# A hybrid decoder block on one core: the first phase of the input projection in five k ranges instead of four

## The reference

```
c_act = silu(c)
mod = c_act @ ada_w[l] + ada_b[l]                  # 2048 x 12288
sh1, sc1, g1, sh2, sc2, g2 = split(mod, 6)
u = rms_norm(x, mix_norm_pre[l]) * (1.0 + sc1) + sh1
proj = u @ w_in                                     # 2048 x 16384
rq, rk, rv, rg, mq, mk, mv, ga, gb = split(proj)
```

## Time and profile before

| | us |
|---|---|
| median of 3 runs | 1830.6 |
| lowest and highest | 1830.5, 5219.44 |
| the profiled execution | 1830.5 |
| its span | 1828.5 |
| its mean granted TensorE clock | 0.996 of full speed |

### The profile page before, as it was taken

One profiled execution on the slowest core, in us unless ns is written; L12 is line 12 of the kernel. 1 busy time (PEld: TensorE's weight loads), 2 busy tenths in 40 slices (PEclk: granted clock), 3 DMA queues, 4 the chain that ended last, 5 costly groups with the idle time before them and its releaser, 6 DMA issues.

```text
span 1828.5 us, 26196 instructions
## 1 busy us (share of the span) xinstructions
PE 1803.9 (99%) x8980; PEld 1530.1 (84%) x8980; DVE 1377.5 (75%) x1973; ACT 857.2 (47%) x991; POOL 189.6 (10%) x269
## 2 busy tenths in 40 slices
PE   8999999999999999999999999999999999999998
PEld 6777888888888888888888878888888888888886
DVE  6998788978888788888997576777777776744555
ACT  4444544444454545463445455444444444444444
POOL 0000022222222222222210000000000000000000
PEclk8999999999999999999999999999999999999999
DMA  9999688978888887879886636555555555555552
GB/s 353 387 387 349 186 272 271 289 236 273 271 259 273 257 288 243 288 234 305 276 272 216 209 119 203 185 184 189 193 191 184 184 191 193 188 187 202 185 196 103
DMA packets 304595, 432.96 MB, mean 237 GB/s; under 512 B 50724, under 2 KB 174292, under 8 KB 303888
## 3 DMA queue, kind: packets, MB, share of 16 engines
q1 hardware_dynamic: 244304, 360.77, 59.7%
q0 software_dynamic: 20736, 67.34, 10.5%
q10 hardware_dynamic: 39488, 3.96, 1.7%
HBM read 429.79 MB, written 2.23 MB: 236 GB/s over the span
## 4 chain that ended last, share of the span: by engine, by line
PE 91%; DVE 5%; DMA 1%; issue 1%; ACT 1%; SPq 0%; DVEq 0%; ACTq 0%
PE ps L929 18%; PE ps L559 12%; PE ps L561 12%; PE ps L560 12%; PE ps L590 10%; PE ps L937 9%; PE ps L995 4%; PE ps L997 4%; PE ps L996 4%; DVE ada_acc L1539 2%; DVE w_low L1440 1%; PE ps L598 1%; DVE ada_acc L1521 1%; DMA stage<-in_w_in 1%; DMA ada_first<-in_ada_w 1%
## 5 line engine op out<-in xcount | busy, mean ns | idle before, releaser
L1440 DVE TENSOR_TENSOR w_low<-stage,w_high 128x1024 fp32r<-128x1024 f32 x608 | 743.0, 1223 | 378.2 <-ACT w_high L1041 363.9
L1041 ACT ACTIVATE w_high<-stage 128x1024 fp32r<-128x1024 f32 x552 | 583.7, 1060 | 724.0 <-PE ps L561 273.8
L559 PE MATMUL ps<-w_high,lhs 128*128 128x512 f32 x992 | 389.6, 393 | 0.0
L561 PE MATMUL ps<-w_high,lhs 128*128 128x512 f32 x992 | 386.3, 389 | 0.0
L560 PE MATMUL ps<-w_low,lhs 128*128 128x512 f32 x992 | 386.1, 389 | 0.0
L929 PE MATMUL ps<-lhs,w_high 128*128 128x512 f32 x1408 | 336.7, 391 | 0.5 <-DVE lhs L1488 0.5
L929 PEld LDWEIGHTS ps<-lhs,w_high 128*128 128x128 f32 x1408 | 258.6, 188 | 50.7 <-DVE lhs L1488 0.8
L543 POOL DMA_DIRECT2D ada_ring<-in_ada_w x256 | 185.1, 723 | 755.6 <-DVE ada_acc L1464 538.3
L1464 DVE SCALAR_TENSOR_TENSOR ada_acc<-ada_ring,c_act,ada_acc 128x256 f32<-128x256 f32 x480 | 230.4, 480 | 18.8 <-DMA ada_ring<-in_ada_w 8.7
L561 PEld LDWEIGHTS ps<-w_high,lhs 128*128 128x128 f32 x992 | 186.2, 188 | 39.1
L560 PEld LDWEIGHTS ps<-w_low,lhs 128*128 128x128 f32 x992 | 186.3, 188 | 38.1
(11 more groups left out here) (211 smaller groups left out, 1485.8 us busy)
## 6 DMA issues: line engine op xcount, KB each, us to landing
stage<-in_w_in SPq DMA_DIRECT2D x100, 1024.0 KB, 7.0
stage<-in_ffn_w_up SPq DMA_DIRECT2D x176, 512.0 KB, 4.3
ada_ring<-in_ada_w POOLq DMA_DIRECT2D x256, 256.0 KB, 5.6
stage<-in_ffn_w_down SPq DMA_DIRECT2D x44, 1024.0 KB, 5.0
ada_first<-in_ada_w SPq DMA_DIRECT2D x64, 512.0 KB, 11.3
stage<-in_w_in SPq DMA_DIRECT2D x56, 512.0 KB, 11.4
stage<-in_ret_w_o SPq DMA_DIRECT2D x16, 1024.0 KB, 6.8
stage<-in_moba_w_o SPq DMA_DIRECT2D x16, 1024.0 KB, 6.9
```

The lines of the kernel that those rows point to most:

```text
L559: pe.matmul(acc, hi, w_high[:, slot, k, :], start=kt == 0, stop=False)
L561: last = pe.matmul(acc, lo, w_high[:, slot, k, :], start=False, stop=kt == KT - 1)
L1041: act.activation(w_high[:, h % 4, :, :], stage[:, slot, 2 * (h % 2):2 * (h % 2) + 2, :], ACT.Copy).then_inc(high_ready, 1)
L1440: dve.tensor_tensor(w_low[:, h % 4, :, :], stage[:, slot, 2 * (h % 2):2 * (h % 2) + 2, :], w_high[:, h % 4, :, :].bitcast(F32), ALU.subtra ...
```

## The change

`FIRST_PAIRS` becomes five ranges of 1, 1, 2, 2 and 2 pairs. The units of work are now (group, range), written out for each stage, so that a streamed group may be visited for a range that was ready earlier, or for two ranges in a row without leaving its bank. `VISITS` lists the thirteen stays of a streamed group in banks 6 and 7 (sixteen before): four first ones, copied by ACT, and nine that DVE adds, in two additions each. The next range's summation stands behind RK0, the last unit of a stage, and the first unit behind it is of an older range. The shift and scale are made one load earlier (3 behind the unit instead of 4). For a range of one pair a step is 512 columns wide with shift and scale together, and a slot holds four row blocks. In the opening the steps are 256 wide and alternate between the shift half and the scale half, except in the last slot, where the shift half comes first; each waits for the last step of its own half. The warm-up products are 4, 1 and 12 instead of 33, 1 and 10.

```diff
-FIRST_PAIRS = ((0, 1), (2, 3), (4, 5), (6, 7))
+FIRST_PAIRS = ((0,), (1,), (2, 3), (4, 5), (6, 7))
 STAGES = len(FIRST_PAIRS)
-FIRST_ORDER = ((0, 1, 2, 3, RV0, RQ0, RK0),) * (STAGES - 1) + ((RV0, 0, 1, RQ0, 2, 3, RK0),)
-SUM_BEHIND = (RQ0,) * (STAGES - 1) + (None,)
+FIRST_ORDER = (((0, 0), (1, 0), (RV0, 0), (2, 0), (RQ0, 0), (RK0, 0)),
+               ((3, 0), (3, 1), (RV0, 1), (0, 1), (RQ0, 1), (RK0, 1)),
+               ((1, 1), (1, 2), (RV0, 2), (2, 1), (2, 2), (RQ0, 2), (RK0, 2)),
+               ((3, 2), (3, 3), (RV0, 3), (0, 2), (0, 3), (RQ0, 3), (RK0, 3)),
+               ((1, 3), (1, 4), (RV0, 4), (0, 4), (RQ0, 4), (3, 4), (2, 3), (2, 4), (RK0, 4)))
+SUM_BEHIND = tuple((RK0, st) for st in range(STAGES - 1)) + (None,)
...
+VISITS = []
+for _i, (_g, _r) in enumerate(FIRST_UNITS):
+    if _g < 4 and (_i + 1 == len(FIRST_UNITS) or FIRST_UNITS[_i + 1][0] != _g):
+        VISITS.append((_g, _r, _i, all(_v[0] != _g for _v in VISITS)))
...
             for slot in range(ada_slots(0)):
-                for part in ((0, 1), (1, 2)) if slot > 4 else ((0, 2),):
-                    for k in range(ada_rows(0)):
-                        yield slot, k, part
+                pieces = [(k, part) for k in range(ada_rows(0)) for part in range(2)]
+                if slot == ada_slots(0) - 1:
+                    pieces.sort(key=lambda piece: piece[1])
+                for k, part in pieces:
+                    yield slot, k, part
...
-                if n == FIRST_END[st, SUM_BEHIND[st]] + 4:
+                if n == FIRST_END[SUM_BEHIND[st]] + 3:
                     return st + 1
...
                 if st and 0 in which:
-                    n_out(4 * st - 1, 0)
+                    done = FIRST_UNITS.index(SUM_BEHIND[st - 1])
+                    n_out(sum(i <= done for _, _, i, _ in VISITS) - 1, 0)
...
-            def first_streamed(n, st, j, summed):
+            def first_streamed(n, i, j, r, summed):
+                begins, ends = FIRST_UNITS[i - 1][0] != j, FIRST_UNITS[i + 1][0] != j
...
-            keep_warm(33)
+            keep_warm(4)
             sum_first(0, (0,))
             keep_warm(1)
             sum_first(0, (1,))
-            keep_warm(10)
+            keep_warm(12)
...
-                    if i == 0:
+                    if row == 0:
                         op = dve.tensor_scalar(acc, block_, c_act[:, 0:1], None, ALU.mult)
                     else:
-                        dve.wait_ge(ada1_step, i)
+                        dve.wait_ge(ada1_step, last[part] + 1)
```

More of the change, by code:

```diff
@@ L413, in prepares_before, with kept_before @@
             for st in range(STAGES - 1):
-                if n == FIRST_END[st, SUM_BEHIND[st]] + 4:
+                if n == FIRST_END[SUM_BEHIND[st]] + 3:
                     return st + 1
             return None
[L418 to L424, removed]
+        def kept_before(n, first):
+            for v, (j, r, _, is_first) in enumerate(VISITS):
+                if is_first == first:
+                    end = FIRST_END[j, r]
+                    if n == end + (3 if len(FIRST_PAIRS[r]) == 2 else 4):
+                        yield v, j, r, 0
                     if n == end + 4:
-                        yield st, j, 1
+                        yield v, j, r, 1
         def scaled_by(pair, t):
@@ L452, in first_ada, with first_load @@
                                      "(k p) n -> p k n", p=P)).then_inc((ada1_in, ada1_scale_in)[which][q % 4], 16)
[L454 removed]
+            def first_load(n, pair, g):
                 wait(sp, split_ready, n - 7)
@@ L468, in _ @@
             for st in range(STAGES):
-                for g in FIRST_ORDER[st]:
-                    for pair in FIRST_PAIRS[st]:
-                        first_load(n, st, pair, g)
+                for g, r in FIRST_ORDER[st]:
+                    for pair in FIRST_PAIRS[r]:
+                        first_load(n, pair, g)
                         st_, ops = ada_ops_behind(n)
@@ L612, in _, with n_out @@
             pe.wait_ge(warm_set, 2)
[L614 to L619, removed]
+            def n_out(v, t):
+                if v >= 0:
+                    is_first = VISITS[v][3]
+                    before = sum(visit[3] == is_first for visit in VISITS[:v])
+                    pe.wait_ge(n_kept if is_first else n_added, 2 * before + t + 1)
             def sum_first(st, which=(0, 1)):
@@ L691, in first_streamed @@
                             last.then_inc(used, 1)
-                    if t == 0:
+                    if t == 0 and ends:
                         last.then_inc(n_first, 1)
@@ L708, in _ @@
             sum_first(0, (1,))
[L709 removed]
+            keep_warm(12)
             n = 0
[L711 to L723 removed]
+            for i, (g, r) in enumerate(FIRST_UNITS):
+                summed = 1 + sum(unit in SUM_BEHIND for unit in FIRST_UNITS[:i])
+                if i == 0:
+                    first_opening()
+                elif g < 4:
+                    first_streamed(n, i, g, r, summed)
+                else:
+                    first_resident(n, r, g)
+                n += len(FIRST_PAIRS[r])
+                if (g, r) in SUM_BEHIND:
+                    sum_first(summed)
             def ret_side(G):
@@ L1523, in opening_ada @@
                     op.then_inc(ada1_step, 1)
+                    last[part] = i
             def first_ada(st, i):
@@ L1555, in add_streamed @@
             def add_streamed(n):
-                for st, j, t in kept_before(n, range(1, STAGES)):
+                for v, j, r, t in kept_before(n, False):
                     if t == 0:
-                        dve.wait_ge(n_first, 4 * st + j + 1)
+                        dve.wait_ge(n_first, v + 1)
                     else:
-                        dve.wait_ge(used, FIRST_END[st, j] + 1)
+                        dve.wait_ge(used, FIRST_END[j, r] + 1)
                     b = gate_b[:, t, j * NC:(j + 1) * NC]
```

66 lines of the change are left out of this document (27 added, 39 removed).

## The result

The changed kernel takes 1833.85 us (median of 20 runs; without one disturbed run they lie between 1832.7 and 1836.0), the kernel before 1830.6 (within 0.6 of each other, one disturbed run aside). The ratio is 1.0019, 95% interval 1.0013 to 1.0025. The predicted time, 1830.2, was 3.65 us off. The difference is small, 0.19%, but its interval excludes no change, so the forecast of no change (0.4 us to the fast side) did not hold. The profiled execution of the changed kernel took 1835.3 us with a span of 1833.3, 4.8 more than the span before.

The account below looks back on a forecast made before the run. DVE's pace bounds the first phase: its work eats the 11.6 us head start, and the phase ends at 211.7 to 212.3 against 212.0. So -0.3 to +0.3 on 1830.5, said as 1830.2 us; 8 in 10 between 1825 and 1835.

Parts of the forecast that it names:

- ledger of DVE: First phase, range by range: DVE's work summed in one line, PE's time beside it; phase ends at 211.7 against 212.0.
- rival (b): Opening and range 1: alternate halves don't hide the dependence, narrow steps cost more; loss 3.5 to 6.4 us, chance 0.15.
- PE's waits on additions: First phase: PE's 3.9 us of waits on L1563 go, and waits on the last accumulation step take their place.
- head start: Opening: first useful product at 32.5 instead of 44.16, 11.6 us earlier, of which nothing is left at the phase's end.
- The matmuls behind it start half as fast, which DVE's own pace hides.: Behind range 2's summation: clock falls after PE's 6.8 us idle; only the slower summation costs, 1.1 us of DVE waiting.
- Both arrive together: Range 4, ahead of the last summation: DVE's last step ends at 160.3, PE is done at 159.9.
- the 0.7 for a late split: Range 4, PE's pairs ahead of the last summation: 0.7 us added for a late split, and 0.7 once more behind it.
- this cover: Behind each summation: RK0 of the same range, 5.4 us, stood there before; now the summation is behind RK0, a new wait.
- the forecast's own range: Whole kernel: 1828.3 us (the clock holds, 1.1 less, gaps smaller) to 1832; forecast's chance 0.55.
- Rival (c): Transfers: 1 KB rows run a fifth lower, 310 GB/s, 5.4 us more, 4 of it covered; 1831.7 us, chance 0.1.
- a last shift row after 165: End of first phase: last shift expected near 162; before 158 or after 165 would show the forecast wrong.
- Rival (a): First phase: the head start stays, 1818.9 us, or some 4 us of it, 1826.5; chance together 0.2.

Follow-up runs that it names:

- c1: Changed kernel with all but the first accumulation step of each range after the opening covering only 128 columns (work left out): 1828.02 us.
- c3: c1 with the scale half of ada_w also neither loaded nor waited for in ranges 2 to 4: 1817.63 us.
- e5: e1 and e3 together on the changed kernel, with 8 zero-matrix filler products ahead of range 1's summation as well: 1831.64 us.
- r1: Changed kernel run again without an edit, for a second profile: 1834.21 us, profiled run 1834.07.
- e1: Changed kernel plus zero-matrix filler products on PE ahead of the summations of range 2 (28) and range 3 (6): 1831.25 us, ratio to before 1.0004.
- e6: Four ranges of two pairs as before, with the new visits, alternating opening and RK0 behind the summation: 1829.58 us, ratio to before 0.9996.
- e3: Changed kernel with partial sums of one-pair visits taken out one load earlier (3 behind instead of 4): 1833.90 us.
- e4: e3 plus the summation moved back behind RQ0, RK0 running behind it, shift and scale again four loads behind: 1833.84 us.
- e7: e6 with DVE's shift and scale made one split earlier (3 behind instead of 4): 1829.42 us, ratio to before 0.9995.

## Why the prediction was wrong

**The opening and the ledger of DVE held.** Forecast against rows: opening's end 27.6, measured 26.87; shift 28.4, 27.57; range 1's shift 52.6, 53.36; range 2's wait of PE 6.8, measured 6.54; its shift 82.2, 83.53; range 3's 121.2, 122.81. The first useful product came at 31.47 for 32.5. The alternating halves hide the dependence, so rival (b) is excluded. PE's waits on additions became the single one ahead of the third summation, as said. One part of the ledger was short: from shift 0 to shift 1 it had 24.2 us and 25.8 passed, 1.2 of the difference being DVE's waits of 0.78 and 0.39 us for ACT's conversions at 40.9 and 46.7. With the 0.6 and 0.3 of the next two ranges, and 0.8 won in the opening, this makes shift 3 come 1.6 late. That the head start leaves no trace because DVE sets the pace was right as far as it went; c1 shows that it was only the first of two bounds, since the transfers would have held it too, and c3 shows the start coming through once both are off.

**The step that failed** is the one behind the clock's fall: "The matmuls behind it start half as fast, which DVE's own pace hides." For range 2 this was nearly true: the ten half-speed products were hidden, for PE waited 1.48 us for DVE at the next summation all the same. (The summation itself, at half clock, held DVE for 1.27 us, which the forecast had as 1.1; in e5, with the clock full there, the shift of range 2 stands at 82.54, 1.0 earlier.) The forecast named one fall, where PE waited longest, and then let the clock be full for the rest. The trace has two more that count, behind the summations of ranges 3 and 4, where PE waited 1.48 us and not at all. Three things follow in the sum.
- Range 4 in the forecast: PE at 159.9, DVE at 160.3, "Both arrive together". Measured: DVE's last steps end at 162.4 (160.3 plus the 1.6 that it was late at shift 3, and 0.5), PE's summation ends with the shift at 166.03 and DVE waits 2.43 for it. PE's forecast of 159.9 has to be raised by the late start, 1.6, by a gap of 0.4 (see below) and by 14 half-speed products, 2.8, that the sum had at nothing; the 0.7 for a late split comes off, for PE waited for none here. This gives 164.0. PE's summation starts at 164.16 and ends at the shift. With only 0.4 us of slack between the two engines in the forecast, nothing hid the 2.8.
- Behind the last summation nothing hides anything either: 1.2 us in the first profile, 0 in the second.
- The gap of 0.37 us on L702, four times. Now a streamed unit stands right behind the summation and writes bank 6, which the summation has just used, so PE waits until DVE has read it. Before, RK0 stood there. The forecast said that this cover was gone, and priced only the wait ahead of the summation, not the gap behind it. The one behind the fourth summation is in the sum above, the one behind the last comes on top, 0.4; DVE's pace hides the first two.

So the last summation starts 3.9 later than the 160.3 of the forecast, and 1.2 and 0.4 come behind it, less 0.4 of the 0.7 that the forecast set there for a late split (in r1 it cost 0.3): 211.7 + 5.1 = 216.8, where the mark says 212.0 + 5.05 = 217.1. e1 tells the shares apart better: without the falls at ranges 3 and 4 the time is 2.6 us lower. The 0.7 that then remain to the kernel before are not clear of nothing by e1's interval, and no run divides them among the gaps, the late shift 3 and the rest. The change itself brings the late shift and the gaps whatever the clock does, and e6 shows that with four ranges the visits cost nothing.

**The range and the rivals.** The median lies inside the stated range of 1825 to 1835, but in its upper part, and outside the forecast's own range, which ended at 1832. Rival (c) named the transfers: their rate was lower, 363 instead of 387 GB/s in the opening, where the forecast had added nothing. That is 6%, not the fifth that the rival took. PE's idle time of 2.6 us behind ACT's late copy was real and, by e3, hidden. ACT's late loads also held DVE for the 1.2 us named above; e3 leaves these loads as they are, so that part is not tested. The forecast had named a last shift row after 165 as a sign of being wrong; it stands at 166.03. Rival (a), a kept head start, 1818.9 or 1826.5, is excluded by the result.

The sentence on the clock gate in the Trainium skill ("TensorE: Matmul & The Clock Gate", on HAM oscillation) explains a fall by one long wait between bursts. The trace agrees for the wait of 6.54 us. It does not cover the other two: the fall at 123 us came after a wait of 1.48, and that at 167 after a gap of 0.37 alone. Only the one-column products of a summation, 1.84 to 2.04 us of them, stood beside it. The measurement decides here: the forecast looked for a fall only where PE waited long, and so left these two out of the sum.

## What to carry to other kernels

When a step of tiny matmuls (here sixteen of one column) is moved from in front of dense resident work to in front of a gap, ask for each place at which it stands what the clock does behind it, not only at the place with the longest wait, and price it at 0.20 us for every 512-column product at half clock. Dense work behind the step helped at most places here, but not at all of them (e4 at 117 us). Then ask whether the engine beside it has slack at that place: the half-speed products cost nothing behind 84 us, where DVE was late, and nearly the full price behind 123 and 167, where PE was. And where a forecast says that two engines arrive together, each small term that was set to nothing for either of them can be on the path.

## What the runs showed of the hardware that was not expected

- The clock's fall is not settled by the wait alone. Two profiles with the same 1.84 us wait ahead of the same summation show granted clocks of 0.66 and 1.00 behind it (e6, e7), and two profiles of one kernel show 0.57 and 1.00 behind the last summation. The runs of the changed kernel scatter over 3.4 us where those of the kernel before scatter over 0.6; r1 shows 1.2 of the 3.4 to be the clock's, the rest is not shown. One profile of such a kernel shows one draw. What decides the draw is open; no run here was made for it.
- The place of a fall can differ between two executions of one kernel: the changed kernel had one at 37 to 41 us in its first profile, and one at 54 to 57 in r1. e5 has the pattern of r1 and e1 that of the first profile, so what e5's eight additional fillers did to it cannot be told.
- Transfers with 1 KB rows beside others ran at 363 GB/s from 24 to 43 us. In e6, with 2 KB rows in the same stretch, it was 386, and the stretch of the earlier trace rows, also 1 KB rows, had shown 385. Which difference between the two kinds of 1 KB rows makes the 6% is open.
